# Attention: one VectorE add for both key tiles of a step, and the next head's low parts made by GpSimd

## The chip, the cores and the metric

The kernel runs on one core of a Trainium2 chip. The metric is the device time of one execution in microseconds (us); the kernel before took 3183.33 us as the median of 3 runs (3180.16 to 3183.79). Five engines work side by side and meet only at semaphores: TensorE (PE in the profile, its weight loads PEld), VectorE (DVE), ScalarE (ACT), GpSimd (POOL) and SyncE (SP, which here only issues transfers).

## The reference, cut to what matters

The program computes a whole trunk layer (modulated norm, convolution branch, latent attention, gates, routed experts). The change lies in the attention: 8 heads, keys and queries of 64+32 channels, values of 64.

```
s = q_nope @ k_nope^T + q_rope @ k_rope^T
p = softmax(s * (64 + 32) ** -0.5)
o = p @ v
```

There are 2048 sample tokens (2304 keys: 256 cached and 2048 own) and 256 prompt tokens, which attend to their own 256 keys.

## The kernel before, in words

**Precision.** Every key and query array is split in two: a high part, which is the value rounded to the matmul's type, and a low part, which is the value less the high part. A score is the sum of three matmuls, high by high, low by high, high by low (lines 1233 to 1235). ACT makes the high parts (line 1139). The low parts are made by subtraction. For head 0 POOL does it ahead of the loop (line 1186); for each later head DVE does it during the head before, in 8 pieces: four key pieces of 64 partitions by 640 columns and four query pieces of 96 by 576 (function `split`, line 1315). The pieces come at steps 4, 6, 9, 11, 14, 16, 19 and 21 of a head (the table `AT`), for ACT and for DVE alike.

**Steps.** A head has 37 steps: four query blocks of 512 tokens with 9 steps each, and the prompt block of 256 tokens with one. A step g covers 256 keys as two tiles of 128 keys, k = 0 and 1. 37 is odd, so steps that are even in the program's count in one head are odd in the next.

**One iteration** of PE's loop takes two steps, g and g+1 (lines 1292 to 1306): the scores of g; the maximum products of step g+12 (line 1262; plain scores in [query, key] layout, of which DVE finds the row maxima, line 1322); the scores of g+1; the maximum products of g+13; and the value products of steps g-2 and g-1 (line 1274). Where one of these two steps is the last of its block, its value products are followed by the sum products (line 1283). They multiply `part` by ones, which gives the softmax denominators of the block. PE goes through this order without a choice, so a wait anywhere holds all that follows.

**Weights and `part`.** ACT takes exp of each score tile into `w`, a ring of 4 steps with two tiles each (line 1160). `part[:, j % 2, k]` holds, for block j, the running sum over steps of tile k's weights. Tile 0's half is added up by DVE (line 1349, semaphore `add_d`), tile 1's half by POOL (line 1210, semaphore `add_p`), one operation of 128 x 512 each in a step. A block's first step has no operation of its own (the second adds two `w` tiles); the prompt block's single step is a copy (lines 1346 and 1207). ACT may write over a tile of `w` when the add that read it is done, and PE waits for both semaphores ahead of a block's sum products (lines 1279 and 1280).

**DVE's order in an iteration** (lines 1373 to 1394): two maxima of step g+12, now and then a row of negated maxima for a later block (line 1332), the adds of steps g-2 and g-1, two maxima of step g+13, and then the low pieces that are due. POOL's order: the adds, and now and then the low part of a convolution or output weight (line 1197, 128 x 1024).

**SP** loads the next head's keys and queries (lines 1066 to 1073). It does so once the head before last's low pieces are made, so that the raw buffer is free, and behind the stores of the last block of the head before and the reload of its sums, which stand ahead in its queue.

Of the kernel before, what the change touches and what calls it, by code (L numbers as in the profile page):

```python
# [37 lines left out]
H = 8  # L38
# [880 lines left out]
def attention_phase(nc, t, V, ident, raw, c_ld, room, other, wc_hi, wc_lo, wo_hi, wo_lo):  # L919
# [72 lines left out]
    with ExitStack() as ctx:  # L992
# [20 lines left out]
        add_d, add_p = p.sem("add_d"), p.sem("add_p")  # L1013
# [38 lines left out]
        with nc.Block() as block:  # L1052
# [77 lines left out]
            def _(act):  # L1130
# [22 lines left out]
                for g, (h, b, c) in enumerate(STEPS):  # L1153
                    n = BLOCKS[b][1]
                    for k in range(2):
                        act.wait_ge(s_mm, 2 * g + k + 1)
                        if g >= NW:
                            act.wait_ge(pv_mm, g - NW + 1)
                            act.wait_ge((add_d, add_p)[k], adds_over(g - NW))
                        act.activation(w[:, g % NW, k, 0:n], sc[:, (2 * g + k) % SCB, 0:n], ACT.Exp, scale=SM_SCALE  # L1160
                                       ).then_inc(exp_done, 1)
# [20 lines left out]
            def _(pool):  # L1182
                for i, r in enumerate(FIRST):
                    pool.wait_ge(hi_piece, i + 1)
                    src, hi, lo = piece(0, r, slice(0, HQ))
                    pool.tensor_tensor(lo, src, hi.bitcast(F32), ALU.subtract).then_inc(lo_first, 1)
# [5 lines left out]
                for g, (h, b, c) in enumerate(STEPS):  # L1192
# [5 lines left out]
                    if not joins(g):  # L1198
                        continue
                    j, n = block_of(g), BLOCKS[b][1]  # L1200
                    pool.wait_ge(exp_done, 2 * g + 2)
                    if c < 2:
                        wait(pool, sum_mm, j - 1)
                    else:
                        pool.wait_ge(add_p, ADDS[g])
                    if is_last(g) and c == 0:
                        pool.tensor_copy(part[:, j % 2, 1, 0:n], w[:, g % NW, 1, 0:n]).then_inc(add_p, 1)
                    else:
                        before = w[:, (g - 1) % NW, 1, 0:n] if c == 1 else part[:, j % 2, 1, 0:n]
                        pool.tensor_tensor(part[:, j % 2, 1, 0:n], before, w[:, g % NW, 1, 0:n], ALU.add).then_inc(add_p, 1)  # L1210

            @block.tensor
            def _(pe):
# [52 lines left out]
                def values(g):  # L1266
# [11 lines left out]
                    if is_last(g):  # L1278
                        pe.wait_ge(add_d, ADDS[g + 1])
                        pe.wait_ge(add_p, ADDS[g + 1])  # L1280
# [30 lines left out]
            def _(dve):  # L1311
                def split(h, r, rows=slice(0, NOPE)):
                    dve.wait_ge(hi_piece, PIECES * h + r + 1)
                    src, hi, lo = piece(h % 2, r, rows)
                    dve.tensor_tensor(lo, src, hi.bitcast(F32), ALU.subtract).then_inc(lo_piece, 1)

# [18 lines left out]
                def add(g):  # L1335
# [4 lines left out]
                    dve.wait_ge(exp_done, 2 * g + 1)  # L1340
                    if c < 2:
                        wait(dve, sum_mm, j - 1)
                    else:
                        dve.wait_ge(add_d, ADDS[g])
                    if is_last(g) and c == 0:
                        dve.tensor_copy(part[:, j % 2, 0, 0:n], w[:, g % NW, 0, 0:n]).then_inc(add_d, 1)
                    else:
                        before = w[:, (g - 1) % NW, 0, 0:n] if c == 1 else part[:, j % 2, 0, 0:n]
                        dve.tensor_tensor(part[:, j % 2, 0, 0:n], before, w[:, g % NW, 0, 0:n], ALU.add).then_inc(add_d, 1)  # L1349
# [23 lines left out]
                for g in range(0, G, 2):  # L1373
# [15 lines left out]
                    for i in (g, g + 1):  # L1389
                        h = STEPS[i][0]  # L1390
                        if i % PER == 12 and h:
                            invert(h - 1)
                        if i % PER in AT and h + 1 < H:
                            split(h + 1, AT[i % PER])
# [1542 lines left out]
```

## Time and profile before

| | |
|---|---|
| median of 3 runs | 3183.33 us (3180.16 to 3183.79) |
| the profiled execution's own time | 3184.42 us |
| its span | 3182.6 us |
| attention (950 to 1862 us of the span) | 912 us |
| PE busy over the span | 92% |
| DVE, ACT, POOL busy over the span | 61%, 34%, 33% |
| granted PE clock, mean | 0.955 |

The page of the profile lists the busy time of each engine, 40 slices of the span, and the costliest groups of instructions with the idle time ahead of them and what ended it. The timeline lists instructions in order of time: start, duration, engine, line, operation, count. Instructions of one line that follow each other are merged, and the duration is then from the first one's start to the last one's end. The attention is the stretch that the change touches.

### The profile page before, as it was taken

The page shows a single profiled execution, that of the slowest core. Times are in us where ns is not written, and L with a number is a line of the kernel's source. Part 1 is how long each engine was busy: PE and PEld are TensorE (multiplying, and loading weights), DVE is VectorE, ACT ScalarE, POOL GpSimd, SP SyncE. Part 2 cuts the span into 40 slices and gives each one's busy share as a digit, 9 for nine tenths or more (in the row PEclk, how much of TensorE's full clock was granted, in tenths as well). Part 3 has the DMA queues.
Part 4 walks back from the last instruction along what each step waited for, and adds up shares of the span by engine and source line. Part 5 has one row for each costly group of instructions (what it writes and reads, how often), then busy time and mean ns, then how long its engine had stood idle before and what let it go on. Part 6 is the DMA issues. An engine that isn't in the chain of part 4 may idle for free. (4 is left out here: it accounts for less than half of the span.)

```text
span 3182.6 us, 43970 instructions
## 1 busy us (share of the span) xinstructions
PE 2928.4 (92%) x16924; PEld 2348.9 (74%) x16924; DVE 1934.8 (61%) x2561; ACT 1084.9 (34%) x1718; POOL 1061.3 (33%) x686
## 2 busy tenths in 40 slices
PE   6999999999789999999999979979954999999993
PEld 2888888888667777777777757768834888888882
DVE  4418393839347777777777746545674555555565
ACT  4411111111344444444444423213422344343434
POOL 0000000000123343444333535421214766666652
PEclk8999999999889999999999999989976999999996
DMA  5312222211540101110110136574414566666667
GB/s 210 109 54 105 76 105 80 105 64 67 177 140 10 27 19 26 25 33 13 27 25 6 60 94 205 173 242 163 158 54 141 184 199 204 202 212 200 207 187 281
DMA packets 139524, 371.26 MB, mean 117 GB/s; under 512 B 20886, under 2 KB 47996, under 8 KB 129116
## 3 DMA queue, kind: packets, MB, share of 16 engines
q1 hardware_dynamic: 99820, 266.47, 25.3%
q0 software_dynamic: 23984, 74.71, 8.3%
q10 hardware_dynamic: 15552, 27.79, 2.5%
q8 instruction: 110, 1.80, 0.2%
q14 instruction: 58, 0.48, 0.0%
HBM read 265.99 MB, written 102.89 MB: 116 GB/s over the span
## 5 line engine op out<-in xcount | busy, mean ns | idle before, releaser
L1160 ACT ACTIVATE at_w<-at_sc 128x512 f32<-128x512 f32 (+1 forms) x592 | 346.3, 591 | 417.8 <-PE at_sc L1235 362.8
L1322 DVE TENSOR_REDUCE at_mpart<-at_mx 128x2 f32<-128x512 f32 x575 | 368.5, 683 | 167.0 <-PE at_mx L1262 166.9
L1210 POOL TENSOR_TENSOR at_part<-at_part,at_w 128x512 f32<-128x512 f32 x224 | 297.4, 1328 | 359.4 <-ACT at_w L1160 356.1
L2479 POOL TENSOR_TENSOR moe_gu_lo<-moe_raw_gu,moe_gu_hi 128x2048 fp32r<-128x2048 f32 x64 | 296.6, 4635 | 121.7 <-ACT moe_gu_hi L2545 121.3
L520 DVE SCALAR_TENSOR_TENSOR fr_r<-fr_r,fr_dw 128x2334 f32<-128x2334 f32 x120 | 318.0, 2650 | 3.9
L377 PE MATMUL fr_po<-hT_hi,fr_w_hi 128*128 128x512 f32 (+1 forms) x800 | 297.1, 371 | 3.1 <-PE fr_po L377 1.9
L377 PE MATMUL fr_po<-hT_hi,fr_w_lo 128*128 128x512 f32 (+1 forms) x800 | 294.7, 368 | 0.0
L377 PE MATMUL fr_po<-hT_lo,fr_w_hi 128*128 128x512 f32 (+1 forms) x800 | 294.6, 368 | 0.0
L1274 PE MATMUL at_acc<-at_w,V 128*64 128x256 f32 (+1 forms) x2368 | 289.7, 384 | 0.0
L2664 DVE TENSOR_TENSOR moe_d_lo<-moe_raw_d,moe_d_hi 128x1024 fp32r<-128x1024 f32 x64 | 184.1, 2876 | 105.3 <-ACT moe_d_hi L2576 105.3
L1349 DVE TENSOR_TENSOR at_part<-at_part,at_w 128x512 f32<-128x512 f32 x224 | 228.9, 1022 | 19.7 <-ACT at_w L1160 6.7
L1274 PEld LDWEIGHTS at_acc<-at_w,V 128*64 128x64 f32 x2368 | 156.9, 137 | 84.3 <-ACT at_w L1160 2.1
L248 POOL DMA_DIRECT2D fr_wm<-w_ada_rows x32 | 16.8, 530 | 525.2 <-PE fr_acc L402 525.2
L291 ACT ACTIVATE fr_r<-fr_po 128x512 f32<-128x512 f32 (+1 forms) x100 | 55.5, 555 | 388.2 <-PE fr_po L377 388.2
L377 PEld LDWEIGHTS fr_po<-hT_hi,fr_w_hi 128*128 128x128 f32 x800 | 151.0, 189 | 37.7 <-issue 12.1
L377 PEld LDWEIGHTS fr_po<-hT_lo,fr_w_hi 128*128 128x128 f32 x800 | 150.9, 189 | 25.3
L377 PEld LDWEIGHTS fr_po<-hT_hi,fr_w_lo 128*128 128x128 f32 x800 | 151.0, 189 | 25.1
L2756 PE MATMUL moe_g<-moe_x_hi,moe_gu_hi 128*128 128x288 f32 x512 | 158.9, 310 | 8.2 <-POOL moe_gu_lo L2479 5.4
L2756 PE MATMUL moe_g<-moe_x_hi,moe_gu_lo 128*128 128x288 f32 x512 | 152.3, 297 | 0.0
L2756 PE MATMUL moe_g<-moe_x_lo,moe_gu_hi 128*128 128x288 f32 x512 | 152.1, 297 | 0.0
L2756 PE MATMUL moe_u<-moe_x_hi,moe_gu_hi 128*128 128x288 f32 x512 | 151.5, 296 | 0.0
L2756 PE MATMUL moe_u<-moe_x_hi,moe_gu_lo 128*128 128x288 f32 x512 | 151.0, 295 | 0.0
(391 smaller groups left out, 6800.5 us busy)
## 6 DMA issues: line engine op xcount, KB each, us to landing
moe_raw_gu<-w_gate_up SPq DMA_DIRECT2D x64, 1024.0 KB, 4.8
moe_raw_d<-w_down SPq DMA_DIRECT2D x64, 512.0 KB, 5.2
fr_wm<-w_ada_rows POOLq DMA_DIRECT2D x32, 512.0 KB, 4.1
gates_scratch<-fr_r ACTq DMA_DIRECT2D x64, 256.0 KB, 2.0
mx_gates<-gates_scratch SPq DMA_DIRECT2D x64, 256.0 KB, 3.1
fr_raw<-w_in SPq DMA_DIRECT2D x28, 512.0 KB, 5.1
fr_r<-x POOLq DMA_DIRECT2D x18, 512.0 KB, 4.6
raw<-mixed_scratch SPq DMA_DIRECT2D x9, 1024.0 KB, 6.2
```

Source lines behind the costliest of these rows:

```text
L248: pool.dma_start(wm[:, n % 2].rearrange("p h n -> p (h n)"), t["w_ada_rows"][n]).then_inc(wm_ld[n % 2], 16)
L291: act.activation(stage[:, n % PO, 0:size], po[:, n % PO, 0:size], ACT.Sigmoid if KINDS[j] == "g" else ACT.Copy).then_inc(out_done, 1)
L377: mm = pe.matmul(out[:, 0:size], w[:, s, k, :], h[:, k, tok:tok + size], start=first, stop=final)
L520: dve.scalar_tensor_tensor(out=conv, in0=v[:, w:w + CW], scalar=scalar, in1=conv, op0=ALU.mult, op1=ALU.add).then_inc(taps, 1)
L1160: act.activation(w[:, g % NW, k, 0:n], sc[:, (2 * g + k) % SCB, 0:n], ACT.Exp, scale=SM_SCALE).then_inc(exp_done, 1)
L1210: pool.tensor_tensor(part[:, j % 2, 1, 0:n], before, w[:, g % NW, 1, 0:n], ALU.add).then_inc(add_p, 1)
L1274: mm = pe.matmul(acc[half * DV:(half + 1) * DV, j % 2, 0:n], V[:, h, key_tiles(b, c) + k, :], w[:, g % NW, k, half * n:(half + 1) * n], st ...
L1322: dve.tensor_reduce(mpart[:, s, 2 * half:2 * half + 2, c], max_bank(m, half), AX.X, ALU.max).then_inc(red_done, 1)
L1349: dve.tensor_tensor(part[:, j % 2, 0, 0:n], before, w[:, g % NW, 0, 0:n], ALU.add).then_inc(add_d, 1)
L2479: pool.tensor_tensor(gu_lo[:, slot], raw_gu[:, slot], gu_hi[:, slot].bitcast(F32), ALU.subtract).then_inc(glo_done, 1)
L2664: dve.tensor_tensor(d_lo[:, slot], raw_d[:, m], d_hi[:, slot].bitcast(F32), ALU.subtract).then_inc(dlo_done, 1)
L2756: mm = pe.matmul(bank[g][:, 0:TOK], w[:, slot, g, k], x[:, u, k], start=(k == 0 and w is gu_hi and x is x_hi), stop=(k == KD - 1 and x is ...
```

## The change

One operation of DVE adds both tiles of a step, and takes over what POOL did. The semaphores `add_d` and `add_p` become one, `add_done`; ACT and PE wait on that. DVE's add now waits for both exponentials of its step. The eight low pieces of the next head move from the end of DVE's iteration to POOL, at the same steps of the table `AT`; they still count `lo_piece`.

```diff
@@ ACT, before an exponential
-                            act.wait_ge((add_d, add_p)[k], adds_over(g - NW))
+                            act.wait_ge(add_done, adds_over(g - NW))
@@ POOL
+                def split(h, r):
+                    pool.wait_ge(hi_piece, PIECES * h + r + 1)
+                    src, hi, lo = piece(h % 2, r, slice(0, NOPE))
+                    pool.tensor_tensor(lo, src, hi.bitcast(F32), ALU.subtract).then_inc(lo_piece, 1)
...
-                    if not joins(g):
-                        continue
-                    j, n = block_of(g), BLOCKS[b][1]
-                    pool.wait_ge(exp_done, 2 * g + 2)
-                    if c < 2:
-                        wait(pool, sum_mm, j - 1)
-                    else:
-                        pool.wait_ge(add_p, ADDS[g])
-                    (copy or add of part[:, j % 2, 1, 0:n], then_inc(add_p, 1))
+                    l = g % PER
+                    if l in AT and h + 1 < H:
+                        split(h + 1, AT[l])
@@ PE, before the sum products
-                        pe.wait_ge(add_d, ADDS[g + 1])
-                        pe.wait_ge(add_p, ADDS[g + 1])
+                        pe.wait_ge(add_done, ADDS[g + 1])
@@ DVE
-                    dve.wait_ge(exp_done, 2 * g + 1)
+                    dve.wait_ge(exp_done, 2 * g + 2)
                     if c < 2:
                         wait(dve, sum_mm, j - 1)
                     else:
-                        dve.wait_ge(add_d, ADDS[g])
+                        dve.wait_ge(add_done, ADDS[g])
                     if is_last(g) and c == 0:
-                        dve.tensor_copy(part[:, j % 2, 0, 0:n], w[:, g % NW, 0, 0:n]).then_inc(add_d, 1)
+                        dve.tensor_copy(part[:, j % 2, :, 0:n], w[:, g % NW, :, 0:n]).then_inc(add_done, 1)
                     else:
-                        before = w[:, (g - 1) % NW, 0, 0:n] if c == 1 else part[:, j % 2, 0, 0:n]
-                        dve.tensor_tensor(part[:, j % 2, 0, 0:n], before, w[:, g % NW, 0, 0:n], ALU.add).then_inc(add_d, 1)
+                        before = w[:, (g - 1) % NW, :, 0:n] if c == 1 else part[:, j % 2, :, 0:n]
+                        dve.tensor_tensor(part[:, j % 2, :, 0:n], before, w[:, g % NW, :, 0:n], ALU.add).then_inc(add_done, 1)
...
-                        if i % PER in AT and h + 1 < H:
-                            split(h + 1, AT[i % PER])
```

(The line in brackets stands for the four lines of code at 1206 to 1210.)

## Rows read from the trace of the kernel before

**Rows 1.** Windows view, the attention: length, busy time of each engine, clock.
```profile
core 0: us, PE busy (x) PEld busy (x) DVE busy (x) ACT busy (x) POOL busy (x), PEclk, DMA share, GB/s
950.00:1862.00 912.00, 900.04 (x5724) 666.38 (x5722) 690.41 (x979) 406.34 (x689) 363.51 (x272) 0.99 0.10 25
```
**Rows 2.** Waits in the attention: who waited for whom, us, times, longest.
```profile
ACT at_w L1160 <- DVE at_part L1349: 28.1, 16, 2.0
PEld at_sc L1233 <- ACT at_w L1160: 12.0, 18, 2.0
...
DVE room L1315 <- ACT room L1139: 9.7, 3, 3.5
...
PEld at_mx L1248 <- DVE at_mpart L1322: 1.6, 4, 0.4
...
PEld at_acc L1283 <- DVE at_part L1349: 0.7, 1, 0.7
PEld at_mx L1262 <- DVE at_mpart L1322: 0.5, 2, 0.2
```
**Rows 3.** DVE's groups in the attention: busy us, mean ns, idle before.
```profile
L1322 DVE TENSOR_REDUCE at_mpart<-at_mx 128x2 f32<-128x512 f32 x564 | 361.6, 683 | 165.8 <-PE at_mx L1262 165.7
L1349 DVE TENSOR_TENSOR at_part<-at_part,at_w 128x512 f32<-128x512 f32 x224 | 228.9, 1022 | 19.7 <-ACT at_w L1160 6.7 <-DVE at_part L1349 0.5
L1315 DVE TENSOR_TENSOR at_k_lo<-raw,other 64x640 fp32r<-64x640 f32 x16 | 13.0, 810 | 8.1 <-ACT other L1139 8.1
```
**Rows 4.** Timeline where POOL's and DVE's adds overlap: start, duration.
```profile
1051.20 1.29 POOL L1210 TENSOR_TENSOR at_part<-at_part,at_w 128x512 f32<-128x512 f32 x1 [1.43 <-ACT at_w L1160]
1051.96 2.92 DVE L1349 TENSOR_TENSOR at_part<-at_part,at_w 128x512 f32<-128x512 f32 x2
1053.06 1.27 POOL L1210 TENSOR_TENSOR at_part<-at_part,at_w 128x512 f32<-128x512 f32 x1 [0.58 <-ACT at_w L1160]
```
**Rows 5.** A DVE add of 128 x 1024 in a later phase: min/median/max ns.
```profile
L2043 DVE TENSOR_TENSOR op_y<-op_y,op_x x18: 1224/1225/1227, 2125.1 to 2342.1; 128x1024 f32<-128x1024 f32 x18
```
**Rows 6.** Timeline, a block that ends in its iteration's second step.
```profile
1150.33 1.48 DVE L1349 TENSOR_TENSOR at_part<-at_part,at_w 128x512 f32<-128x512 f32 x2
1151.12 1.49 PEld L1274 LDWEIGHTS at_acc<-at_w,V 128*64 128x64 f32 x16
1151.43 1.50 POOL L1210 TENSOR_TENSOR at_part<-at_w 128x512 f32<-128x512 f32 x1 [4.07 <-ACT at_w L1160]
1151.72 1.28 DVE L1322 TENSOR_REDUCE at_mpart<-at_mx 128x2 f32<-128x512 f32 x2
1152.68 0.79 PEld L1283 LDWEIGHTS at_acc<-at_part,at_ones 128*64 128x64 f32 x8
```
**Rows 7.** Timeline, the same in head 0, where PE waited.
```profile
1008.62 0.67 DVE L1349 TENSOR_TENSOR at_part<-at_part,at_w 128x512 f32<-128x512 f32 x1
1009.75 1.70 DVE L1349 TENSOR_TENSOR at_part<-at_part,at_w 128x512 f32<-128x512 f32 x1 [0.46 <-ACT at_w L1160]
1011.51 0.63 PEld L1283 LDWEIGHTS at_acc<-at_part,at_ones 128*64 128x64 f32 x8 [0.69 <-DVE at_part L1349]
```
**Rows 8.** POOL's subtractions for head 0: busy us, mean ns.
```profile
L1186 POOL TENSOR_TENSOR room<-raw,room 96x640 fp32r<-96x640 f32 x4 | 6.1, 1550 | 29.0 <-ACT room L1139 29.0
...
L1186 POOL TENSOR_TENSOR room<-raw,room 96x576 fp32r<-96x576 f32 x4 | 5.6, 1426 | 0.0
```
**Rows 9.** Timeline, head 1, first block's end, with step 9's piece.
```profile
1091.94 0.19 PEld L1233 LDWEIGHTS at_sc<-other 97*128 97x128 f32 x1 [0.39 <-issue]
1094.15 0.73 ACT L1139 ACTIVATE room<-raw 64x640 fp32r<-64x640 f32 x1
1095.10 1.48 DVE L1349 TENSOR_TENSOR at_part<-at_part,at_w 128x512 f32<-128x512 f32 x2
1097.45 0.57 PEld L1283 LDWEIGHTS at_acc<-at_part,at_ones 128*64 128x64 f32 x6
```
**Rows 10.** Timeline, head 1, second block's end, with step 19's piece.
```profile
1124.56 0.68 ACT L1139 ACTIVATE room<-raw 96x576 fp32r<-96x576 f32 x1
1125.51 1.07 DVE L1349 TENSOR_TENSOR at_part<-at_part,at_w 128x512 f32<-128x512 f32 x1
1126.99 0.79 PEld L1283 LDWEIGHTS at_acc<-at_part,at_ones 128*64 128x64 f32 x8
```
**Rows 11.** Windows view around 1310 us (same columns as rows 1).
```profile
1300.00:1310.00 10.00, 8.90 (x53) 6.43 (x49) 4.17 (x7) 3.16 (x7) 2.56 (x2) 1.00 0.61 131
1310.00:1313.00 3.00, 2.50 (x9) 1.99 (x11) 2.86 (x6) 2.22 (x5) 1.42 (x2) 0.58 0.49 110
1313.00:1316.00 3.00, 3.00 (x16) 1.65 (x16) 3.00 (x4) 0.40 (x1) 1.12 (x1) 0.50 0.00 0
```

More of the change, by code:

```diff
@@ L1012, in attention_phase @@
         s_mm, exp_done, pv_mm, sum_mm = (p.sem(n) for n in ("s_mm", "exp_done", "pv_mm", "sum_mm"))
-        add_d, add_p = p.sem("add_d"), p.sem("add_p")
+        add_done = p.sem("add_done")
         m_mm, red_done = p.sem("m_mm"), p.sem("red_done")
@@ L1197, in _ @@
                         pool.tensor_tensor(lo, wraw[:], hi.bitcast(F32), ALU.subtract).then_inc(w_lo_done, 1)
-                    if not joins(g):
-                        continue
-                    j, n = block_of(g), BLOCKS[b][1]
-                    pool.wait_ge(exp_done, 2 * g + 2)
-                    if c < 2:
-                        wait(pool, sum_mm, j - 1)
-                    else:
-                        pool.wait_ge(add_p, ADDS[g])
[L1206 to L1210, printed above, removed]
+                    l = g % PER
+                    if l in AT and h + 1 < H:
+                        split(h + 1, AT[l])
             @block.tensor
@@ L1311, in _ @@
             def _(dve):
[L1312 to L1315, printed above, removed]
                 def reduce_max(m):
```

## The prediction

> **What bounds the kernel now.** I read the windows view over the attention first. PE is busy 900.0 of 912 us at a clock of 0.99, DVE 690, ACT 406, POOL 364 [rows 1]. So PE is the bound, and a change on DVE and POOL counts only where it makes PE wait or takes a wait of PE away. The list of waits comes second. PE's weight loads waited 12.0 us for ACT, and for DVE 1.6, 0.7 and 0.5 us [rows 2]. All that a perfect DVE could give back is therefore under 3 us. The 12.0 us for ACT lie where ACT stands before the next head's keys, which are still on their way. That transfer is issued behind the last block's stores in SP's queue, and the change moves nothing there. The large figures, DVE waiting 166 us for maximum products [rows 3] and ACT 28.1 us for an add [rows 2], are idle time of engines with time to spare. The third view is the timeline around each block's end. There PE must have the finished `part` and has no other work, so there a slower add shows.
>
> **The adds, in total.** Before, DVE's add of 128 x 512 takes 1.02 us in the mean [rows 3], but 0.69 us undisturbed: two in a row take 1.48 [rows 6], that is 0.69 + 0.10 for the wait of the second on the first + 0.69. The rest is POOL: an add that starts while POOL's runs ends 0.55 us behind POOL's end. The pair of 2.92 us shows it: POOL's second add ends at 1054.33, DVE's pair at 1054.88 [rows 4]. After, an add is 128 x 1024. The trace has no such add into `part`. Bounds: 0.69 us, if the doubled length were free, and 1.38, twice the short one. I take 1.225, the DVE add of the same length with both inputs in SBUF [rows 5]. Then DVE's adds grow from 256 x 1.02 = 261 us to 256 x 1.225 = 314, and 56 pieces of about 0.8 leave it, 45 us. DVE stays at about 700 of 912 us, and its total bounds nothing. What changes is the pair: from 1.48 undisturbed (2.92 at worst) to 1.225 + 0.10 + 1.225 = 2.55 us each time.
>
> **The blocks' ends.** The sum products of a block whose last step is the second of its iteration need both adds of the pair. Undisturbed the pair starts at 1150.33, and PE comes to the sum products at 1152.68, 2.35 us later; before, it had ended 0.87 us early [rows 6]. After, it ends at 1150.33 + 2.55 = 1152.88, and PE goes on 0.06 us behind a finished add (1009.75 + 1.70 = 1011.45, PE at 1011.51 [rows 7]): at 1152.94, a wait of 0.26. There are 11 such ends with no piece in the way. In five the distance is 2.35, in six 2.25 to 2.27, where the wait is 0.35: 5 x 0.26 + 6 x 0.35 = **3.4 us**. At the bounds of the add the wait is 0 or 0.6 each, so this term lies between 0 and 6.6. In head 0, PE already waited 0.69 us, as POOL had come ahead of the second add [rows 7]. PE was there at 1010.82; after, the pair ends at 1008.62 + 2.55 = 1011.17, and the wait is 0.41: **-0.3 us**. Ends on an iteration's first step need one add: rows 10 leave 1.48 us for 1.225 + 0.06, so they hold where nothing is in the way. The prompt block's copy of 2 x 256 columns costs between 0.29 and 0.69 us by its half and by the 128 x 512 add, and has over 1.1 us.
>
> **The pieces on POOL.** A piece of 64 x 640 is not in the trace on POOL; 96 x 640 takes 1.55 us and 96 x 576 1.43 [rows 8]. Bounds for 64 x 640 are 1.28 (POOL's 128 x 512 [rows 4]) and 1.55; I take 1.55, its column count. POOL starts 0.08 us behind ACT's high part. PE needs the pieces only a head later, so their own time is free. Not free is that they hold DVE's adds as POOL's adds did. In even heads, pieces at even steps meet adds too, but at no block's end. In heads 1, 3 and 5 two pieces fall on an end:
> - Step 9 [rows 9]. ACT's part ends at 1094.88, POOL runs 1094.96 to 1096.51. DVE's pair would start at 1095.10, is held, and its first add ends 0.55 + 0.53 = 1.08 behind POOL (the 0.55 of the short add and 512 more columns, 1.225 - 0.69), at 1097.59. The second ends 0.10 + 1.225 later, 1098.92, and PE goes on at 1098.98 instead of 1097.45: 1.5 us, three times, **4.5 us**. If DVE came first, POOL would hold the second add and the end be the same. If a piece held no add, it would be 0.26 each, 0.8.
> - Step 19 [rows 10]. POOL runs 1125.32 to 1126.75, the single add ends at 1127.83, PE goes on at 1127.89 instead of 1126.99: 0.9 us, three times, **2.7 us**; 0 if a piece held no add.
>
> The Trainium skill, page SBUF — State Buffer, section "Who interferes with whom", makes the read interface that the two engines share an exclusive lock: the DVE operation with two SBUF inputs or the GpSimd operation that reads SBUF, whichever starts later, is blocked until the other is finished. The trace agrees: DVE's short add ends 0.55 us behind POOL's end. By that rule the two items come to 7.2 us; without it, to 0.8.
>
> **What is queued behind the held adds.** DVE's two maxima of step g+13. PE reuses their banks two and more products later, in the next iteration. Scores start at 1091.94 and ACT's piece at 1094.15, 2.2 us later [rows 9]. A held pair ends 4.8 us behind the piece's start, the first maximum behind it at 5.4; PE wants that bank about 5.3 behind (5.8 us from iteration to iteration, 1.7 to the bank, less 2.2). So 28 pieces at even steps cost 0 to 0.1 us each; I take 0 and keep up to 3. ACT's exponentials that wait for an add (16 times, 28.1 us [rows 2]) start 0.15 us later, and 1.2 us later at step 22 of heads 1, 3 and 5. PE needs the first of them 1.4 us later than it has it now, so 0. The wait for the second exponential of a step costs nothing: it was done an iteration ago.
>
> **Gains.** DVE no longer stands before ACT's part (9.7 us at three heads' starts [rows 2]), but PE waits for ACT itself there. One wait fewer for PE at 40 sums: below what two transitions in the timeline let me tell, 0 to 1 us in all; I take 0.
>
> **Sum.** 3.4 - 0.3 + 4.5 + 2.7 = 10.3 us. The profiled execution's own time is 3184.4 (span 3182.6 and 1.8 around it), so 3194.7. It lies 1.1 above the median of the runs, so against that the forecast is **3193.6 us**.
>
> **Rivals.**
> - *The pieces hold no add where it matters* (the race at steps 9 and 19 falls otherwise, or an operation on 64 partitions holds it less). For it: all depends on 0.14 us between POOL and DVE. Against: the order of the two does not alter the end. Then 3.4 - 0.3 + 0.8 = 3.9: 3187.2. Chance 0.22.
> - *No wait reaches PE*, since the pairs start earlier once DVE has no pieces, or the add is shorter. For it: it takes only 0.3 us at most ends. Against: the pair's start follows PE's own maximum products, with and without a piece ahead (distance 2.27 and 2.35). 3183.3. Chance 0.18.
> - *Faster, by the clock.* In head 3, PE stands 2.0 us before ACT at 1308.5, and from 1310 to 1316 the granted clock is 0.58 and 0.50, half speed [rows 11]: about 3.1 us lost. In heads 1 and 5 it stands 1.4 and 1.8 us, and the clock stays. If the waits at the blocks' ends stay out and this stand shrinks below about 1.8 us, since DVE, free of pieces, hands adds to ACT earlier, the 3.1 come back and with them up to 2.8 of PE's waits for DVE [rows 2]: 3177.4. Against: the stand ends with the keys' transfer. Chance 0.09.
> - *Slower by the clock.* The new waits of 1.5 us in heads 1, 3 and 5 bring such a drop each, 3.1 us, from a stand of about 1.8 to 2.0 us on: 3193.6 + 9.3 = 3202.9. Against: single stands of 1.8 did not. Chance 0.09.
>
> My forecast has the remaining 0.42; alone it ranges from 3189 to 3198.
>
> **How the numbers follow.** A measurement of this kernel tells 0.2%, 6.4 us, from no change, so the bounds are 3177 and 3189.7. Slower: 0.42 + 0.09, and a few of the first rival's cases above its middle, less my forecast's lower edge, 0.52. Faster: the third rival and part of the second, 0.1. Same: 0.38. The range reaches down to just under the second rival and up to the last one: 3181 to 3202.
>
> **What would show it.** In the timeline after: adds of 1.22 us, in pairs of 2.5; POOL pieces of 1.4 to 1.6 us, and an add that starts inside one ends 1.08 us behind it. In the waits, PE's sum products for DVE's add: about 18 waits, 10 to 11 us in place of 0.7, with 1.5 us in heads 1, 3 and 5 at the first block's end and 0.9 at the second's. In the windows view, the attention at 922 us and all else as before. It is wrong if the sum products wait under 3 us in total, if a piece inside an add's time leaves it at 1.22, or if PE waits longer at another line (1262, 1233).

## The result, and the profile after

| | before | after |
|---|---|---|
| median (range, runs) | 3182.57 us (3180.16 to 3183.79, 4) | 3203.35 us (3198.81 to 3208.58, 4) |
| profiled execution, its span | 3184.42, 3182.6 us | 3200.83, 3199.0 us |
| first score to last sum product of the attention | 921.7 us | 931.2 us |
| first to last down product of the experts | 674.0 us | 680.4 us |

The ratio is 1.0067, with 1.005 to 1.0084 as its 95% interval. The medians differ by 20.8 us where 10.3 were forecast, and the time lies 1.4 us above the range. The two profiled executions differ by 16.4 us: 9.5 in the attention, 6.4 in the expert phase, where no line was changed, and 0.5 between and around them.

**The attention went as worked out.** The page and the windows view of after (columns as in rows 1):

```profile
L1338 DVE TENSOR_TENSOR at_part<-at_part,at_w 128x1024 f32<-128x1024 f32 x224 | 297.4, 1328 | 18.7 <-ACT at_w L1160 6.0
```
```profile
950.00:1862.00 912.00, 899.11 (x5687) 661.26 (x5687) 725.52 (x919) 406.79 (x689) 115.83 (x64) 0.99 0.10 25
```

DVE is busy for 726 us where it had 690 [rows 1], and POOL's work falls from 364 to 116. Both still lie under PE. The loss stands in the waits of PE in this stretch (who waited for whom, us, times, longest):

```profile
PEld at_acc L1277 <- DVE at_part L1338: 11.8, 18, 1.6
PEld at_sc L1228 <- ACT at_w L1160: 11.7, 17, 2.8
...
PEld at_mx L1257 <- DVE at_mpart L1311: 3.4, 7, 0.8
PEld at_mx L1243 <- DVE at_mpart L1311: 2.9, 8, 0.6
```

Against [rows 2], the sum products' wait is 11.8 us in place of 0.7, 11.1 more. The forecast had 10.3 more, in "about 18 waits, 10 to 11 us". The two waits for maxima grew from 1.6 and 0.5 to 2.9 and 3.4, so by 4.2 us. PE's waits for ACT stayed as they were. That the attention as a whole grew by 9.5 and not by 15.3 has two parts that rows show. A wait of a weight load is not all a wait of the products behind it: PE's own wait at the sums is 4.9 us, and its idle time between products grew by 6.9 us over the attention, from 8.4 to 15.3. And the time lost to a lower granted clock fell from 15.9 to 13.9 us (each stretch of the attention at half clock, counted half). These 2.0 us have nothing to do with the change: they lie at the attention's very start, where the clock rose to 1.00 at 959 us before and at 955 after, ahead of the first sum product. The side-by-side table behind kernel 11 takes this loss out.

Timeline of after at the three kinds of block end (start, duration): an ordinary one, step 9 of head 1, step 19 of head 1:

```profile
1151.62 2.54 DVE L1338 TENSOR_TENSOR at_part<-at_part,at_w 128x1024 f32<-128x1024 f32 x2
1154.22 0.63 PEld L1277 LDWEIGHTS at_acc<-at_part,at_ones 128*64 128x64 f32 x8 [0.32 <-DVE at_part L1338]
```
```profile
1093.62 1.56 POOL L1186 TENSOR_TENSOR room<-raw,room 64x640 fp32r<-64x640 f32 x1 [7.87 <-ACT room L1139]
1093.77 3.83 DVE L1338 TENSOR_TENSOR at_part<-at_part,at_w 128x1024 f32<-128x1024 f32 x2
...
1097.65 0.63 PEld L1277 LDWEIGHTS at_acc<-at_part,at_ones 128*64 128x64 f32 x8 [1.60 <-DVE at_part L1338]
```
```profile
1125.87 1.43 POOL L1186 TENSOR_TENSOR room<-raw,room 96x576 fp32r<-96x576 f32 x1 [8.88 <-ACT room L1139]
...
1126.07 2.31 DVE L1338 TENSOR_TENSOR at_part<-at_part,at_w 128x1024 f32<-128x1024 f32 x1
...
1128.43 0.63 PEld L1277 LDWEIGHTS at_acc<-at_part,at_ones 128*64 128x64 f32 x8 [0.95 <-DVE at_part L1338]
```

The undisturbed pair is 2.54 long (2.55 worked out) and PE waits 0.32 (0.26 to 0.35). At step 9, POOL ends at 1095.18. The first add of the pair then ends 1097.60 - 1.22 - 0.10 = 1096.28, 1.10 behind it, and PE waits 1.60. At step 19, POOL ends at 1127.30 and the single add at 1128.38, 1.08 behind, and PE waits 0.95. The forecast had 1.08, 1.5 and 0.9. This is the rule of the Trainium skill, page SBUF — State Buffer, section "Who interferes with whom", that was weighed there, at work on 64 and on 96 partitions.

**The expert phase, which the forecast left out.** Two experts at the start and two at the end are written out; the twelve between are a loop of six passes of two. It takes 511.3 us before and 519.0 after, 7.7 more (from the first of its index copies to the first one behind it). In the middle a pass takes 85.2 us before and 86.8 after (from the second gather's start to that of the next pass). In each pass only one of the two experts differs. First before, then after, the same stretch of one pass, with DVE's copy of the gather indices, POOL's gathers and both engines' subtractions (`d_lo`, `gu_lo`, `h_lo`):

```profile
2701.59 0.17 DVE L2609 COPY moe_idx_g<-tab 128x4 uint32 x1 [0.49 <-issue]
2702.61 1.00 POOL L2462 DMA_INDIRECT moe_xg<-h_scratch,moe_idx_g  x1 [5.87 <-DVE moe_idx_g L2609]
2703.91 0.96 POOL L2462 DMA_INDIRECT moe_xg<-h_scratch,moe_idx_g  x1 [0.30 <-issue]
2703.92 1.25 DVE L2664 TENSOR_TENSOR moe_d_lo<-moe_raw_d,moe_d_hi 128x1024 fp32r<-128x1024 f32 x1 [2.16 <-ACT moe_d_hi L2576]
2705.17 0.86 POOL L2462 DMA_INDIRECT moe_xg<-h_scratch,moe_idx_g  x1 [0.30 <-issue]
2706.06 4.63 POOL L2479 TENSOR_TENSOR moe_gu_lo<-moe_raw_gu,moe_gu_hi 128x2048 fp32r<-128x2048 f32 x1
2709.05 1.93 DVE L2678 TENSOR_TENSOR moe_h_lo<-moe_hid,moe_h_hi 128x256 fp32r<-128x256 f32 x1 [0.48 <-ACT moe_h_hi L2584]
2710.90 4.63 POOL L2479 TENSOR_TENSOR moe_gu_lo<-moe_raw_gu,moe_gu_hi 128x2048 fp32r<-128x2048 f32 x1 [0.21 <-ACT moe_gu_hi L2545]
```
```profile
2712.42 0.17 DVE L2596 COPY moe_idx_g<-tab 128x4 uint32 x1 [0.61 <-issue]
2713.43 1.00 POOL L2449 DMA_INDIRECT moe_xg<-h_scratch,moe_idx_g  x1 [5.99 <-DVE moe_idx_g L2596]
2714.64 1.23 DVE L2651 TENSOR_TENSOR moe_d_lo<-moe_raw_d,moe_d_hi 128x1024 fp32r<-128x1024 f32 x1 [2.05 <-ACT moe_d_hi L2563]
2714.74 1.96 POOL L2449 DMA_INDIRECT moe_xg<-h_scratch,moe_idx_g  x1 [0.31 <-issue]
2717.00 0.86 POOL L2449 DMA_INDIRECT moe_xg<-h_scratch,moe_idx_g  x1 [0.30 <-issue]
2717.87 9.18 POOL L2466 TENSOR_TENSOR moe_gu_lo<-moe_raw_gu,moe_gu_hi 128x2048 fp32r<-128x2048 f32 x2
2719.76 7.58 DVE L2665 TENSOR_TENSOR moe_h_lo<-moe_hid,moe_h_hi 128x256 fp32r<-128x256 f32 x1 [0.48 <-ACT moe_h_hi L2571]
...
2730.18 0.30 PEld L2713 LDWEIGHTS moe_py<-moe_d_hi,moe_h_hi 128*128 128x128 f32 x2 [0.77 <-DVE moe_yo L2622]
```

Read it from the top. DVE's copy of the gather's indices has an issue gap of 0.61 us ahead of it, not 0.49. The gathers start as much later, while `d_lo` follows ACT and does not. Before, the second gather starts 0.01 us ahead of `d_lo`. After, `d_lo` starts 0.10 ahead, and the gather's issue takes 1.96 us in place of 0.96. POOL is then 1 us late for `gu_lo`, so the next `gu_lo` finds its input ready and follows with no gap. In before a gap of 0.21 us was there, and DVE's held `h_lo` got in. In after it does not get in, and a subtraction that takes 0.42 us at 2709.38 of the same trace takes 7.58, across both of POOL's. PE waits for what stands behind it in DVE's queue. In such a stretch PE is busy less: before (2692 to 2734 us) and after (2702 to 2744 us), columns as in rows 1:

```profile
2691.90:2733.90 42.00, 41.88 (x294) 36.82 (x293) 24.48 (x24) 16.52 (x23) 27.00 (x10) 1.00 0.66 204
```
```profile
2702.20:2744.20 42.00, 40.69 (x279) 35.90 (x278) 28.32 (x23) 15.30 (x21) 27.14 (x10) 1.00 0.66 191
```

Five such `h_lo` of 7.57 to 7.63 us stand in after and none in before, where the longest is one of 4.07. The five passes that have one bring nearly all of the loop's 7.7 us. The two experts ahead of the loop gave 1.2 back (91.2 us before, 90.0 after); they take 88.5 to 94.0 us in the thirteen profiles, so the loop is the better measure of what follows.

Why five of six passes, and where the 0.10 us comes from, the records of DVE's own sequencer show, which the views leave out. The index copy is the first DVE operation of the loop's body. Five passes are entered by the loop's backward branch, and from this branch to the next instruction 0.19 to 0.22 us pass in before and 0.29 to 0.34 in after. From there to the copy it is 0.51 us in both. Where the branch is not taken, behind the last pass, the distance is 0.10 in both.

### The profile page after: what moved, and what is told of

It is laid out like the page before. It is cut to its first block and busy times, and to the rows that moved or that the text cites. A ratio compares the mean times of both kernels' runs of the same rounds, so it can differ in the third digit from the quotient of the medians.

```text
span 3199.0 us, 43404 instructions
## 1 busy us (share of the span) xinstructions
PE 2931.3 (92%) x16924; PEld 2346.8 (73%) x16924; DVE 1998.7 (62%) x2505; ACT 1086.1 (34%) x1718; POOL 812.1 (25%) x478
## 5 line engine op out<-in xcount | busy, mean ns | idle before, releaser
L1338 DVE TENSOR_TENSOR at_part<-at_part,at_w 128x1024 f32<-128x1024 f32 x224 | 297.4, 1328 | 18.7 <-ACT at_w L1160 6.0
L2651 DVE TENSOR_TENSOR moe_d_lo<-moe_raw_d,moe_d_hi 128x1024 fp32r<-128x1024 f32 x64 | 190.5, 2976 | 104.7 <-ACT moe_d_hi L2563 104.7
L2743 PE MATMUL moe_u<-moe_x_lo,moe_gu_hi 128*128 128x288 f32 x512 | 150.5, 294 | 0.0
```

The lines of the kernel that those rows point to most:

```text
L1338: dve.tensor_tensor(part[:, j % 2, :, 0:n], before, w[:, g % NW, :, 0:n], ALU.add).then_inc(add_done, 1)
L2651: dve.tensor_tensor(d_lo[:, slot], raw_d[:, m], d_hi[:, slot].bitcast(F32), ALU.subtract).then_inc(dlo_done, 1)
L2743: mm = pe.matmul(bank[g][:, 0:TOK], w[:, slot, g, k], x[:, u, k], start=(k == 0 and w is gu_hi and x is x_hi), stop=(k == KD - 1 and x is ...
```

## The experiments

**1. The adds alone.** One half of the change: DVE adds both tiles, and makes the pieces as before; POOL has nothing of either.

```diff
...
-                    l = g % PER
-                    if l in AT and h + 1 < H:
-                        split(h + 1, AT[l])
...
+                        if i % PER in AT and h + 1 < H:
+                            split(h + 1, AT[i % PER])
```


> DVE adds both tiles in one operation; the eight low pieces stay on DVE and POOL does nothing in a step. Theory (the wait at a block's end is the merged pair's length, 2.55 us, plus what a POOL piece holds): without pieces on POOL, PE's sum products wait about 14 times 0.26 to 0.35 us, some 4 us, with no wait of 0.9 or 1.5 us; attention 3 to 5 us longer than in the kernel before (last sum product about 1860 us against 1855.7). Rival (the single long DVE operation itself and not the lock makes the long waits): sum products wait 11 us here as in the changed kernel. In the expert phase, whose code is untouched: if the 6 us there come from how far POOL's instructions for it are displaced in its stream, this kernel (526 fewer POOL instructions ahead of the loop) may fall either way; if they come from less work on POOL or DVE in the attention, it is slow as well.

3191.39 us (9 runs) against 3184.05, ratio 1.0023 (1.0009 to 1.0038). In its profile the attention takes 924.4 us, 2.7 more than before, and the expert phase 671.2, with no long `h_lo` (its loop 511.2, as in before; the 2.8 us less lie in the two experts ahead of it). Its waits (from 950 us on):

```profile
PEld at_acc L1269 <- DVE at_part L1335: 5.9, 15, 0.8
...
PEld at_mx L1249 <- DVE at_mpart L1308: 2.4, 5, 0.8
...
PEld at_mx L1235 <- DVE at_mpart L1308: 1.4, 4, 0.4
```

So the adds themselves bring 5.2 us of waits at the blocks' ends (5.9 - 0.7), which is the forecast's 3.4 and a little more, and none of the expert phase.

**2. The pieces alone.** The other half: the adds as before on DVE and POOL, the pieces on POOL.

```diff
...
+                    l = g % PER
+                    if l in AT and h + 1 < H:
+                        split(h + 1, AT[l])
                     if not joins(g):
                         continue
...
-                        if i % PER in AT and h + 1 < H:
-                            split(h + 1, AT[i % PER])
```


> The adds stay as before, tile 0 on DVE and tile 1 on POOL; only the eight low pieces move to POOL. Theory: DVE's short pair ends 0.87 us early where nothing holds it, so the eleven ordinary block ends cost nothing; the pieces of steps 9 and 19 of heads 1, 3 and 5 hold DVE's add until 1096.5 and 1126.7 us, and then delay POOL's own adds too, so these six ends wait: POOL's pair of adds behind a 1.55 us piece ends about 2 us after PE comes. Sum products wait 4 to 9 us in all, only in heads 1, 3, 5. Rival (a piece does not hold an add): under 1.5 us. Expert phase: 56 more POOL instructions ahead of the loop, either way by the displacement theory.

3195.4 us (7 runs), ratio 1.0041 (1.0029 to 1.0054). The attention takes 926.6 us, 4.9 more than before; the expert phase 680.5, with five `h_lo` of 7.57 to 7.61 us. Its waits:

```profile
PEld at_acc L1291 <- DVE at_part L1352: 6.5, 6, 1.8
...
PEld at_mx L1256 <- DVE at_mpart L1325: 1.6, 4, 0.4
...
PEld at_mx L1270 <- DVE at_mpart L1325: 0.7, 3, 0.2
```

That is six waits of about 1.1 us, as two ends in each of three heads would give. The two halves' waits at the sums, 5.2 and 5.8 us, add up to 11.0 of after's 11.1. The waits for maxima do not: the pieces alone leave them at 1.6 and 0.7, where before had 1.6 and 0.5. And here is the whole loss of the expert loop (519.0 us). It came with the pieces, not with the adds.

**3. The pieces kept off the blocks' ends.** After, where POOL's pieces at steps 9 and 19 wait for the sum products of the block.

```diff
                     if l in AT and h + 1 < H:
+                        if l in (9, 19):
+                            pool.wait_ge(sum_mm, block_of(g))
                         split(h + 1, AT[l])
```


> The changed kernel, but POOL makes the pieces of steps 9 and 19 only when the sum products of the block before are done, so that no piece lies in front of an add that PE waits for. Theory: the six long waits (1.5 and 0.9 us in heads 1, 3, 5) fall to 0.3 and 0 us, sum products wait about 4 us instead of 11.8, and the attention ends some 6.5 us earlier than in the changed kernel. Rival (the waits of these six come from DVE being late for another reason): they stay. Expert phase: 14 more POOL instructions ahead of the loop than in the changed kernel.

```profile
PEld at_acc L1279 <- DVE at_part L1340: 5.2, 15, 0.4
PEld at_mx L1245 <- DVE at_mpart L1313: 5.1, 9, 2.2
PEld at_mx L1259 <- DVE at_mpart L1313: 3.4, 7, 0.8
```

The sum products' waits fell by 6.6 us (11.8 to 5.2), the longest from 1.6 to 0.4. That is the term of the pieces (4.5 + 2.7 = 7.2), shown by taking it away. The view begins at 930 us here, and over the same stretch after has the same 5.1 and 3.4 us for maxima. They did not move at all, so they do not come from these two pieces. The attention fell by only 2.4 us, to 928.8. In this execution the clock cost 15.8 us, not 13.9, and the products' own waits for ACT at the heads' starts are 1.9 us longer. The time, 3205.23 us (5 runs, ratio 1.0058, 1.0038 to 1.0078), can't be told from after's: a gain of a few us in the profile is under what these runs resolve. The expert phase stayed long, 681.9 (loop 519.0).

**4. Is it the place of POOL's instructions?** After has 470 instructions fewer on POOL ahead of the experts. This kernel is after with 471 semaphore increments on POOL, spread over the attention.

```diff
...
+                    for _ in range(2 if g < 175 else 1):
+                        pool.sem_inc(pad, 1)
```


> The changed kernel with 471 semaphore increments on POOL (which is idle there) spread over the attention steps, so that POOL has 888 instructions ahead of the expert loop as in the kernel before; they compute nothing. Displacement theory (POOL starts its second gather of the odd experts 0.1 us later since its instructions lie elsewhere in the stream, and so falls behind DVE's subtraction): the gathers take 0.96 us again, the five DVE operations of 7.6 us are gone, the expert phase is 677 us long again instead of 684, and the whole about 3193 to 3195 us. Rival (the shift comes from PE's or DVE's streams, or from where the attention leaves the engines in time): expert phase 683 to 690 us, whole about 3200 us. The attention is as in the changed kernel, its waits 11 to 12 us, in both.

3206.47 us (4 runs), ratio 1.007 (1.0053 to 1.0086); the expert phase 681.8 us, its loop 519.0, with the five long `h_lo` (the 677 and 684 of the expectation are on a ruler about 3 us longer). That theory fell.

**5. Or of DVE's?** In the instruction streams DVE has 2568 ahead of the expert phase in before and in kernel 1, and 2512 in after and in kernels 2 to 4: 56 fewer, the pieces' waits and what belongs to them. Short and long expert phases fall apart along that line. This is after with 56 semaphore increments on DVE in the attention.

```diff
...
+                    if g < 112:
+                        dve.sem_inc(pad, 1)
```


> The changed kernel with 56 semaphore increments on DVE, one at the end of each of its first 56 iterations, so that DVE has 2568 instructions ahead of the expert loop as in the kernel before and as in the kernel with the adds alone; they compute nothing. So far the expert phase is short (671 to 674 us from first to last product of the down projection) in the two kernels with 2568, and long (680 to 682) in the four with 2512. Theory (the place of DVE's instructions in its stream decides whether its subtraction starts ahead of POOL's second gather): phase 671 to 675 us, gathers of 0.96 us, no DVE operation of 7.6 us, whole about 3193 us, attention as in the changed kernel. Rival (the work that DVE no longer does, or the pieces on POOL, decide, and not the place): phase 680 to 682 us with five operations of 7.6 us, whole about 3203 us.

The expert phase takes 675.6 us, its loop 511.3 as in before, and no `h_lo` is longer than 2.85. The attention kept its 11.8 us of waits at the sums. In the timeline the gather is ahead of `d_lo` again:

```profile
2717.30 0.17 DVE L2599 COPY moe_idx_g<-tab 128x4 uint32 x1 [0.49 <-issue]
...
2719.62 0.96 POOL L2452 DMA_INDIRECT moe_xg<-h_scratch,moe_idx_g  x1 [0.30 <-issue]
2719.62 1.25 DVE L2654 TENSOR_TENSOR moe_d_lo<-moe_raw_d,moe_d_hi 128x1024 fp32r<-128x1024 f32 x1 [2.16 <-ACT moe_d_hi L2566]
...
2724.75 1.94 DVE L2668 TENSOR_TENSOR moe_h_lo<-moe_hid,moe_h_hi 128x256 fp32r<-128x256 f32 x1 [0.48 <-ACT moe_h_hi L2574]
```

3198.79 us (5 runs), ratio 1.0044 (1.0027 to 1.0061), against 1.0067 and, in a repeat (11), 1.0053 for after. About 3193 was expected. The intervals overlap, so it is the trace that shows this, not the time.

**6. The same the other way.** Before, with 200 semaphore increments on DVE in the attention, one or two an iteration; nothing else is touched.

```diff
...
+                    for _ in range(2 if g < 104 else 1):
+                        dve.sem_inc(pad, 1)
```


> The kernel before with 200 semaphore increments on DVE spread over its iterations in the attention (200 is 56 less than 256, so that the expert loop lies, within any power of two up to 256 instructions, where the change puts it). They compute nothing. Place theory: the expert phase grows from 674 to 680 us or more, with five DVE operations of 7.6 us, though adds and pieces are as before; the whole about 3191 to 3195 us. Rival (work moved, not place): phase 674 us, whole 3184 to 3187 us. The attention: DVE has a quarter of its time free, so at most 1 to 2 us more.

```profile
2794.96 0.17 DVE L2612 COPY moe_idx_g<-tab 128x4 uint32 x1 [0.59 <-issue]
...
2797.18 1.22 DVE L2667 TENSOR_TENSOR moe_d_lo<-moe_raw_d,moe_d_hi 128x1024 fp32r<-128x1024 f32 x1 [2.05 <-ACT moe_d_hi L2579]
2797.28 1.95 POOL L2465 DMA_INDIRECT moe_xg<-h_scratch,moe_idx_g  x1 [0.30 <-issue]
...
2802.32 7.57 DVE L2681 TENSOR_TENSOR moe_h_lo<-moe_hid,moe_h_hi 128x256 fp32r<-128x256 f32 x1 [0.48 <-ACT moe_h_hi L2587]
```

The attention is as before (921.2 us, no wait at the sums), the expert phase 681.8, 7.8 more (its loop 519.0, 7.7 more), with five `h_lo` of 7.55 to 7.61. 3190.06 us (10 runs) against 3184.01, ratio 1.0018 (1.0007 to 1.0029), a little under the 3191 that was expected. Kernels 5 and 6 together show the cause: instructions that compute nothing, in a phase that they do not lengthen, cost about 6 us in a loop whose first long pass begins some 760 us after that phase's end. In the five passes behind a backward branch the issue gap ahead of the index copy is 0.49 to 0.52 us in before and kernels 1, 5, 7 and 9, and 0.59 to 0.65 in after and kernels 2, 3, 4, 6, 8, 10 and 11. In the first group the loop takes 511.2 to 511.3 us, in the second 519.0, and 515.0 in kernels 8 and 10, which have the wait of kernel 8. There is no exception among the thirteen profiles.

**7. Before, with all pieces two steps later.** It takes up the clock rival's premise: PE stands 2.0 us before ACT at 1308.5, behind ACT's wait for the next keys. Their load is issued 0.39 us behind the reload of the sums (1302.90 and 1303.29). What it waits for by semaphore, the low pieces of the head just ahead of the one that it loads (lines 1067 to 1071, and not those of a head further back), has long been made.

```diff
-AT = {4 + 5 * r // 2: r for r in range(PIECES)}
+AT = {6 + 5 * r // 2: r for r in range(PIECES)}
```


> The kernel before with all eight pieces of the next head two steps later (steps 6 to 23 instead of 4 to 21), for ACT and DVE alike; nothing else. If PE's waits for ACT at the heads' starts (12.0 and 5.1 us in the kernel before) come from ACT standing before the key transfer, as the trace says, they mostly go, and the drop of the clock near 1310 us with them: attention 7 to 11 us shorter, whole about 3174 to 3178 us. Rival (the waits only move, since the transfer's landing is not what ends them, or later pieces delay the next head's first maximum products): no change, 3184 us, or slower. Expert phase 674 us.

Its wait at the scores, and its windows view, against [rows 2] and [rows 11]:

```profile
PEld at_sc L1233 <- ACT at_w L1160: 5.0, 13, 0.4
```
```profile
1300.00:1310.00 10.00, 10.00 (x61) 7.61 (x58) 5.85 (x10) 4.54 (x9) 4.07 (x4) 1.00 0.57 122
1310.00:1316.00 6.00, 6.00 (x40) 4.39 (x40) 5.87 (x8) 2.84 (x5) 2.57 (x3) 1.00 0.31 71
```

3174.82 us (10 runs) against 3184.01, ratio 0.9969 (0.9959 to 0.9979): faster than both kernels. The wait fell from 12.0 to 5.0 us, PE's own wait at the scores is gone, and the granted clock stays at 1.00, 2.4 GHz, where its mean had fallen to 0.58 and 0.50, the lower level of 1.2 GHz. The attention takes 909.8 us. The forecast's clock rival named this stand and the 3.1 us behind it; both come back here, by another edit than the one under study. Behind the attention's start the clock does not fall at all in kernels 7, 9 and 10, which have the later pieces, and falls for 1.7 to 3.4 us' worth in all ten other profiles, near 1310 to 1323 us, near 1550, or, in kernel 3, also at 1091. The length of the stand does not settle where it falls, as the forecast took it (1.8 us stays, 2.0 falls): in kernel 6, with before's attention, the clock stayed behind a stand of 2.2 us that ended at 1317 and fell behind one of 1.7 at 1543.

**8. POOL lets DVE in.** After, where POOL's `gu_lo` of part q (each of the 16 experts has four) waits until `h_lo` of part q-2 is done, so that DVE's held operation gets its gap.

```diff
                     pool.wait_ge(ghi_done, q + 1)
+                    if not isinstance(q, int) or q > 1:
+                        pool.wait_ge(hlo_done, q - 1)
```


> The changed kernel; in the expert phase POOL waits ahead of each weight subtraction until DVE's low part of the hidden values two pieces back is made, so that two of POOL's long subtractions cannot follow each other over a DVE operation that waits. Theory (DVE is kept out by two subtractions of 4.6 us in a row): the DVE operations of 7.6 us shrink to under 5 us, PE's wait of 1.2 us in each of the five loop passes goes, and the expert phase is 673 to 677 us instead of 680 to 682, though the second gather still takes 1.96 us where DVE is ahead. Rival (the lost time comes from the gather's own delay): the phase stays at 680 us.

```profile
2715.59 1.94 POOL L2449 DMA_INDIRECT moe_xg<-h_scratch,moe_idx_g  x1 [0.30 <-issue]
...
2720.60 3.02 DVE L2667 TENSOR_TENSOR moe_h_lo<-moe_hid,moe_h_hi 128x256 fp32r<-128x256 f32 x1 [0.48 <-ACT moe_h_hi L2573]
...
2723.70 4.62 POOL L2468 TENSOR_TENSOR moe_gu_lo<-moe_raw_gu,moe_gu_hi 128x2048 fp32r<-128x2048 f32 x1 [0.37 <-DVE moe_h_lo L2667]
```

The gather is still held, and `h_lo` is now 3.02 us long. A pass takes 86.0 us, half-way between 86.8 and 85.2, and the loop 515.0 (519.0 in after, 511.3 in before): 4.0 us of the loss were the long `h_lo`, the other 3.7 come with the late gather. That the whole phase is down to 674.9 us is in part luck, since the two experts ahead of the loop took only 88.6 us. But its time, 3205.07 us (4 runs, ratio 1.0074, 1.0057 to 1.009), is no better than after's, though its profiled execution was its fastest (3198.49). What the other executions lost stays open.

**9. Both on before**: kernel 7 with the wait of kernel 8.

> The kernel before with the pieces two steps later and, in the expert phase, POOL's wait for DVE's low part of the hidden values ahead of each weight subtraction. Theory: the head starts' waits stay gone (attention about 910 to 914 us from first score to last sum product), the expert phase is 671 to 675 us wherever DVE's instructions lie, whole 3172 to 3176 us, better than the kernel before and the changed one. Rival (POOL's new wait holds PE's weights up): expert phase over 677 us and whole over 3178.

3175.77 us (5 runs) against 3185.14, ratio 0.9963 (0.995 to 0.9977); kernel 7 had 0.9969. Where the gather is not late, the wait brings nothing.

**10. The change with all three mends**: pieces two steps later, the one at step 18 behind the sum products, and the wait of kernel 8.

> The changed kernel with everything found so far put right around it: pieces two steps later, the piece of step 18 behind the sum products of the block before, and POOL's wait in the expert phase. What then remains of the change is the longer pair of adds. Theory: against the kernel with the same mendings and the adds as before, the sum products wait 4 to 6 us more in the attention and the rest is equal: whole 3177 to 3182 us. Rival (another cost of the change is still unfound): 3185 us or more.

3188.3 us (10 runs), ratio 1.0004 (0.9994 to 1.0014). It runs level with before and 12.5 us above kernel 9, which differs in the change itself and the step-18 wait. Its expectation of 3177 to 3182 missed, and the rival came in. In the profiles 919.0 against 913.3 us of attention, with 5.1 us of waits at the sums as expected. The expert phase takes 680.6 against 674.4 us, and there the theory had left out what kernel 8 shows: the wait gives back the long `h_lo`, not the late gather, and the loop takes 515.0 against 511.2. These two terms, 5.7 and 3.8, are 9.5 of the 12.5 us; the rest stays open.

**11. After, once more**, beside kernels 9 and 10.

> The changed kernel once more, unchanged, on the same chip as the others, to see how far its parts repeat: sum products wait 11 to 12 us, the expert phase is 680 to 682 us with five DVE operations of 7.6 us; what differs from its first profile is then in the waits for ACT at the heads' starts and in the granted clock. Rival (the expert phase of one program falls either way by chance): 674 us here.

3203.43 us (4 runs) against 3185.14, ratio 1.0053 (1.0038 to 1.0068), or 16.9 us. The medians of the two differ by 18.3. Attention 933.6 us with the same 18 waits and 11.8 us, expert phase 681.7 with the same five `h_lo`, its loop 519.0.

**All side by side.** The second column is the kernel's median less that of before measured beside it. The fourth is the attention less what the lower clock took, an estimate: each stretch at half clock counts half.

| kernel | time, to before | attention | less the clock's loss | expert loop |
|---|---|---|---|---|
| before | | 921.7 | 905.8 | 511.3 |
| after | +20.8 | 931.2 | 917.2 | 519.0 |
| 11 after again | +18.3 | 933.6 | 918.5 | 519.0 |
| 4 (POOL pad) | +22.4 | 934.2 | 918.3 | 519.0 |
| 5 (DVE pad 56) | +14.8 | 934.5 | 918.7 | 511.3 |
| 8 (POOL's wait) | +21.1 | 934.9 | 917.4 | 515.0 |
| 1 (adds) | +7.3 | 924.4 | 912.3 | 511.2 |
| 2 (pieces) | +11.4 | 926.6 | 912.4 | 519.0 |
| 3 (two pieces late) | +21.2 | 928.8 | 913.0 | 519.0 |
| 6 (before, DVE pad 200) | +6.1 | 921.2 | 905.5 | 519.0 |
| 7 (before, later) | -9.2 | 909.8 | 901.3 | 511.3 |
| 9 (before, later, wait) | -9.4 | 913.3 | 899.2 | 511.2 |
| 10 (after, all three) | +3.2 | 919.0 | 904.9 | 515.0 |

Less the clock's loss, the adds alone bring 6.5 us to the attention and the pieces alone 6.6. Both together bring 11.4 to 12.9, in five profiles. With the loop's 7.7 that is 19.1 to 20.4 us for the whole change where nothing is mended, and 18.3 to 22.4 were measured. In the same way kernels 1, 2, 5 and 6 come out within 3 us of their times. Kernels 3 and 8 do not: their times are about 6 us more than their profiles explain.

## Why the prediction was wrong

- **What bounds the kernel: right.** DVE's total rose to 726 of 912 us and bound nothing.
- **The blocks' ends and head 0 (3.4 - 0.3 us): right in mechanism,** low in size. Kernel 1 has 5.9 us in 15 waits, kernel 3 has 5.2 in 15, and before had 0.7 in one.
- **The pieces on POOL (4.5 and 2.7 us): right.** 1.60 and 0.95 us an end were measured where 1.5 and 0.9 were forecast. Moving them away took off 6.6 of the 7.2 us.
- **The maxima queued behind held adds (0, "keep up to 3"): too low.** Their waits grew by 4.2 us. Kernel 1, with the adds alone, has 2.4 us at the maximum products (0.5 before, 3.4 after) and 1.4 us at the turning of the row maxima (1.6 and 2.9). Kernel 2, with the pieces alone, has 0.7 and 1.6. So the longer adds by themselves bring 1.9 us at the products, neither half brings anything at the turning, and nearly all of the other 2.3 us come only with both together. Kernel 3 shows that these are not the pieces of steps 9 and 19. The forecast had named a longer wait at line 1262 as a sign that it is wrong, and this sign came: 3.4 us for 0.5.
- **"In the windows view, the attention at 922 us and all else as before": the step that failed.** (The 922 is rows 1's 912, from 950 us on, plus 10.3; that before's attention from its first score on is 921.7 is chance.) The forecast took the phases behind the attention over unchanged, since none of their lines is touched. In fact before sat there on a lucky order of two starts 0.01 us apart, and the change removed 56 instructions of DVE ahead of that loop. DVE's backward branch then takes 0.10 us more, the index copy issues 0.10 to 0.13 us later, the gather loses the race, and the loop takes 7.7 us more (the phase 6.4 in the first pair of profiles). Kernels 5 and 6 show it in both directions. The forecast's sum plus this term is 10.3 + 7.7 = 18.0 us; 18.3 and 20.8 were measured.
- **The rivals.** None of those named happened. The slow one, with the clock, gives nearly the measured time (3202.9), but for another reason: the clock cost no more after, 13.9 us against 15.9, and behind the new stands of 1.15 us of PE at the blocks' ends of heads 1, 3 and 5 it stayed at 1.00. That it lies so near is luck.

Open: why the place of DVE's instructions in their stream changes the time of the branch. No run here shows what the engine does in it. Other displacements weren't tried, and the two that were, 56 fewer and 200 more, are the same place if only the remainder by 256 counts. Most of the rest between 16.4 us in the profiles and 20.8 between the first medians is no longer open: after's first profile has the shortest attention of five, 931.2 us against 933.6 to 934.9. What kernels 3 and 8 lose besides stays open.

## What to carry to other kernels

When two engines' operations hold each other, merging two short ones on one engine need not shorten the path: here the pair went from 1.48 to 2.55 us at the very places where PE needs its end. Look in every later phase for pairs of such operations that start within 0.1 us of each other, above all in loops, since an edit ahead of them that adds or removes instructions on one of the two engines can turn their order (56 on DVE did, 471 on POOL did not), and price that as a two-way term of the range. Before rearranging engines that have time to spare, look at where the bounding engine itself stands: two steps' shift of the pieces, in one table, was worth 9 us.

## What the runs showed of the hardware

- A waiting two-input DVE operation is not served between two POOL operations that follow each other without a gap: `h_lo` ended behind both, 7.55 to 7.63 us, in after and in kernels 2, 3, 4, 6 and 11, five times each. Where POOL left 0.19 to 0.68 us between the two, it got in each time and ended 0.29 us behind the first of them.
- POOL's issue of an indirect gather takes 0.96 us, and 1.93 to 1.97 where DVE's two-input subtraction started 0.09 to 0.12 us ahead. In kernel 7 such a subtraction had started 0.27 us ahead and the gather took 1.77: in both it ends 0.82 to 0.84 us behind the subtraction's end. So the engines meet at more than semaphores here. The Trainium skill, page SBUF — State Buffer, section "Who interferes with whom", infers that a two-input elementwise operation leaves descriptor generation alone, since it takes only the read interface. These rows speak against taking it so for a gather whose indices lie in SBUF.
- From DVE's backward branch to the next instruction 0.19 to 0.22 us pass with 2568 DVE instructions ahead of the expert phase, and 0.29 to 0.35 with 2512 or 2768. POOL's branch of the same loop has two such levels as well, 0.17 to 0.19 us, and 0.26 to 0.31 in kernels 2, 3, 8 and 10, whose streams on POOL are others.
- The 128 x 1024 add takes 1.22 us undisturbed, both tiles at once, against 2 x 0.69 for the halves: the merging itself saves 0.16 us a step.
